# First four jobs of an fp32 transformer-block kernel on un-normalised input, scaled by 1 / rms afterwards

## The reference, cut to what matters

```
def rms_norm(x, g):
    xf = xf * lax.rsqrt(jnp.mean(xf * xf, axis=-1, keepdims=True) + EPS)
    return xf * g

h = rms_norm(x, norm1_g)                      # x: 256 x 1024
z = h @ w_in                                  # 1024 x 7168
a_val, a_gate = split(z[:, :2048])            # 1024 columns each
a = a_val * sigmoid(a_gate)
a = causal_depthwise_conv(a, conv_w, conv_b)  # 31 taps per channel
a = silu(rms_norm(a, conv_norm_g))
```

## Time and profile before

| | us |
|---|---|
| three runs | 917.16, 919.43, 921.28 (median 919.43) |
| the profiled execution | 918.12 |
| its span | 916.3 |
| PE busy | 877.1 (96% of the span) |
| DVE busy | 639.7 (70%) |
| ACT busy | 553.7 (60%) |
| POOL busy | 344.6 (38%) |

### The profile page before, as it was taken

How to read it: one execution, slowest core, us unless ns; L and a number is a source line. 1 busy time by engine, 2 the same in 40 slices (tenths; PEclk the granted TensorE clock), 3 DMA queues, 4 the chain that set the end, 5 groups by cost and what they waited for, 6 DMA issues and landing times.

```text
span 916.3 us, 18118 instructions
## 1 busy us (share of the span) xinstructions
PE 877.1 (96%) x6794; PEld 837.2 (91%) x6794; DVE 639.7 (70%) x1050; ACT 553.7 (60%) x999; POOL 344.6 (38%) x318
## 2 busy tenths in 40 slices
PE   4999999999999999999999998899999999999996
PEld 3998898888899899999999887898899999999996
DVE  5887998975777798777656679945468854444542
ACT  5667778777646576666455674474545755555441
POOL 2699984435432243333111117520013343333111
PEclk9999999999999999999999999999999999999999
DMA  5655554434556366555756352344245476554641
GB/s 200 207 183 184 178 170 126 143 103 136 147 186 190 100 202 201 180 183 166 229 183 176 127 184 79 107 138 132 76 139 176 148 210 186 183 184 160 209 136 46
DMA packets 42310, 146.41 MB, mean 160 GB/s; under 512 B 4704, under 2 KB 7024, under 8 KB 42224
## 3 DMA queue, kind: packets, MB, share of 16 engines
q1 hardware_dynamic: 41472, 143.67, 50.3%
q10 hardware_dynamic: 752, 1.59, 0.5%
HBM read 144.19 MB, written 1.05 MB: 159 GB/s over the span
## 4 chain that ended last, share of the span: by engine, by line
PE 84%; issue 5%; DVE 4%; ACT 3%; POOL 3%; DMA 1%; DVEq 0%; POOLq 0%; ACTq 0%
PE px L502 25%; PE px L503 24%; PE px L504 24%; PE px L544 3%; POOL att L1973 2%; PE px L564 2%; DVE wlo L1307 1%; PE px L573 1%; PE px L508 1%; PE px L509 1%; PE px L510 1%; PE px L552 1%; ACT whi L842 1%; DVE hx L1328 1%; PE px L566 1%
## 5 line engine op out<-in xcount | busy, mean ns | idle before, releaser
L502 PE MATMUL px<-hx,whi 128*128 128x256 f32 x1392 | 404.0, 290 | 8.7 <-DVE hx L1328 6.1
L503 PE MATMUL px<-hx,whi 128*128 128x256 f32 x1392 | 395.4, 284 | 0.0
L504 PE MATMUL px<-hx,wlo 128*128 128x256 f32 x1392 | 395.3, 284 | 0.0
L1307 DVE TENSOR_TENSOR wlo<-raw,whi 128x1024 fp32r<-128x1024 f32 x251 | 329.9, 1322 | 66.3 <-ACT whi L842 65.3
L842 ACT ACTIVATE whi<-raw 128x1024 fp32r<-128x1024 f32 x267 | 279.9, 1051 | 65.6 <-PE px L504 49.9
L502 PEld LDWEIGHTS px<-hx,whi 128*128 128x128 f32 x1392 | 268.3, 193 | 16.7 <-DVE hx L1328 7.4
L503 PEld LDWEIGHTS px<-hx,whi 128*128 128x128 f32 x1392 | 268.8, 193 | 0.4
L504 PEld LDWEIGHTS px<-hx,wlo 128*128 128x128 f32 x1392 | 268.6, 193 | 0.0
L1863 POOL TENSOR_TENSOR CA<-CA,ct 128x256 f32<-128x256 f32 x90 | 86.7, 963 | 54.5 <-ACT ct L909 47.0
L1930 POOL TENSOR_TENSOR fx<-tt,fx 128x256 fp32r<-128x256 f32 x40 | 56.3, 1410 | 129.7 <-ACT fx L1098 124.5
L503 PE MATMUL px<-fx,whi 128*128 128x256 f32 x352 | 99.6, 283 | 0.0
(11 more groups left out here) (281 smaller groups left out, 1303.1 us busy)
## 6 DMA issues: line engine op xcount, KB each, us to landing
raw<-ws SPq DMA_DIRECT2D x267, 512.0 KB, 3.7
tb<-tabs SPq DMA_DIRECT2D x16, 128.0 KB, 2.9
out<-X SPq DMA_DIRECT2D x4, 256.0 KB, 2.4
X<-xs SPq DMA_DIRECT2D x1, 512.0 KB, 4.9
X<-xs ACTq DMA_DIRECT2D x1, 512.0 KB, 5.0
msk<-lmask ACTq DMA_DIRECT2D x1, 448.0 KB, 3.6
vc<-vecs ACTq DMA_DIRECT2D x1, 319.0 KB, 6.8
ug<-pos ACTq DMA_DIRECT2D x1, 128.0 KB, 4.2
```

The source lines that it names most:

```text
L502: e.matmul(b[:, 0:S], H, xh, start=first, stop=False)
L503: e.matmul(b[:, 0:S], H, xl, start=False, stop=False)
L504: m = e.matmul(b[:, 0:S], L, xh, start=False, stop=end)
L1307: e.tensor_tensor(wlo[:, n % NSL, :], raw[:, n % NRAW, :], whi[:, n % NSL, :], ALU.subtract).then_inc(s_lov, 1)
```

## The change

**Jobs on x times the gain.** The first four jobs (ag0, av0, ag1, av1) no longer read the normalised tiles `hx` but `ax`, which holds x times norm1_g split into high (ACT) and low (DVE) parts. `sums("n1")` moves behind ag0 and av0. When 1 / rms is there, DVE multiplies the four PSUM results by it (`early`), ACT takes the tanh of the two gates, and DVE writes CI(0) and CI(1) (`early_gated`). The later twelve jobs read `hx` as before.

**Pieces.** x comes in four DMAs of two tiles. Chunks 0 and 1 come, and are split, in halves of 128 x 512. All of these are on SP's queue in the order of use, and the 9 columns of vectors that the opening needs come in a small DMA of their own. The other 629 columns come behind chunk 2.

**Engines.** POOL instead of DVE adds up the squares, and chunk 3's low part is DVE's instead of POOL's. The normalised tiles and chunks 4 and 5 are woven together in DVE's and ACT's lists.

ACT's list (the early multiplications and gates are called as shown for DVE):

```
-            e.dma_start(X[:, 0:4, :], xv[:, 0:4, :]).then_inc(s_x[0], 16)
-            e.dma_start(vc[:, :], vecs).then_inc(s_vc, 16)
...
+            for i in range(KD):
+                if i % 2 == 0:
+                    e.wait_ge(s_x[i // 2], 16)
+                e.activation(ax[:, i, 0, :], X[:, i, :], ACT.Copy, scale=vec("norm1_g", i)).then_inc(s_xgh, 1)
+                if i in (1, 3):
+                    half_high(0, i // 2)
+            half_high(1, 0)
+            half_high(1, 1)
+            for i in range(KD):
+                square("n1", i, X[:, i, :])
+                if i == 3:
+                    highs(2)
+            highs(3)
+            rms("n1", D)
...
+            early_gate(0)
+            highs(4)
+            early_gate(1)
```

DVE's list:

```
+            for i in range(KD):
+                e.wait_ge(s_xgh, i + 1)
+                e.scalar_tensor_tensor(out=ax[:, i, 1, :], in0=X[:, i, :], scalar=vec("norm1_g", i), in1=ax[:, i, 0, :],
+                                       op0=ALU.mult, op1=ALU.subtract).then_inc(s_xgl, 1)
+                if i in (1, 3):
+                    half_low(0, i // 2)
...
+            def early(key, to):
+
+                e.wait_ge(s_mm, ENDS[key])
+                e.tensor_tensor(to, px_of[key, 0][:, 0:S], rst[:, 0, 0:S], ALU.mult).then_inc(BANK[key, 0][0], 1)
...
+            e.wait_ge(s_rms, 1)
+            early(("ag", 0), sg[:, 0, :])
+            early(("av", 0), CI[:, 0, 30:])
+            scaled("n1", 0, X[:, 0, :], "norm1_g")
+            early(("ag", 1), sg[:, 1, :])
```

The lists of PE, POOL and SP:

```
+            job(("ag", 0), AX, first_gained, rings=(FEW,))
+            job(("av", 0), AX, rings=(FEW,))
             sums("n1")
+            job(("ag", 1), AX, rings=(FEW,))
+            job(("av", 1), AX, rings=(FEW,))
...
+            for i in range(KD):
+                add_square("n1", i)
             low_tiles("n1", hx)
...
+            tiles(0)
+            half_load(0, 0)
+            tiles(1)
+            half_load(0, 1)
+            tiles(2)
+            tiles(3)
+            half_load(1, 0)
+            half_load(1, 1)
+            loads(2)
+            e.dma_start(vc[:, FIRST_VECS:], vecs[:, FIRST_VECS:]).then_inc(s_vc, 16)
```

More of the change, by code:

```diff
@@ L420, in on_gpsimd, with steps, half, gated_half @@
         def on_gpsimd(c):
-            return c < 64 and c % 4 == 3
+            return 4 <= c < 64 and c % 4 == 3
+        def steps(c):
+            return 2 if c < HALVED else 1
         LOW = {}
         for c in range(n_chunks):
-            n = c // 4 if c < 64 else 16
-            LOW[c] = (s_log, c // 4 + 1) if on_gpsimd(c) else (s_lov, c + 1 - n)
+            mine = [d for d in range(c + 1) if on_gpsimd(d) == on_gpsimd(c)]
+            LOW[c] = (s_log if on_gpsimd(c) else s_lov, sum(steps(d) for d in mine))
+        HI = [sum(steps(d) for d in range(c + 1)) for c in range(n_chunks)]
+        def half(h):
+            return slice(h * CW // 2, (h + 1) * CW // 2)
+        def gated_half(i):
+            return (s_ci, i + 1) if i < 2 else BANK[("av", i), 0]
         ACC = {i: px[3][:, S * (n % 2):S * (n % 2) + S] for n, i in enumerate(CONV_V)}
@@ L831, in _, with half_high @@
         def _(e):
-            made = [0]
+            made = [HALVED]
+            def half_high(n, h):
+                e.wait_ge(s_raw[n] if h else s_half[n], 16)
+                e.activation(whi[:, n, half(h)], raw[:, n, half(h)], ACT.Copy).then_inc(s_hi, 1)
             def highs(c):
```

108 lines of the change are left out of this document (71 added, 37 removed).

## The result

| | before | after |
|---|---|---|
| time, us, median (range) | 919.23 (917.16 to 921.28), 4 runs | 929.28 (928.82 to 929.73), 4 runs |
| ratio | | 1.0112, 95% interval 1.0091 to 1.0133 |
| span of the profiled execution | 916.3 | 927.1 |
| granted clock, mean | 0.996 | 0.988 |

The forecast was 917.5, range 914.0 to 920.7. The kernel is slower by 1.1%, and the forecast was wrong in sign and size. PE's work grew by little: 881.0 us against 877.1.

The account below looks back on a forecast made before the run. PE was taken as the bound, with POOL setting the first head sum: PE's gain of 4.4 us was cut to 1.1 (2.0 - 0.9), giving 917.0 or, on the median, 918.3; forecast 917.5, range 914.0 to 920.7.

Parts of the forecast that it names:

- The second wait at the head sums: PE's wait of 0.5 us at 110 us, for the fifth head sum, was to stay as before.
- the view that decides: PE's waits between 20 and 120 us: one row, 1.9 us in front of `head_sums`, where PE waits for POOL.
- The gain of this change is by how much POOL's tap of 35.23 comes forward: POOL's second tap was to come at 33.2, 2.0 us ahead; less 0.9 inside POOL's run, the gain was 1.1.
- The signs that the prediction named: Times to check in the changed profile, including ones-matmuls near 15.5, sixteenth job's end near 60, POOL's first q square near 94.4.
- 1 / rms at 17.7: In the opening: last addition at 15.5, ones-matmuls' end at 16.7, then Ln and Exp; 4.8 us later than before.
- the clock rival: At the first head sum PE's longer wait drops the clock, costing 1.7 to 2.5 us; time 919.1, chance 0.10.
- DVE's list behind 1 / rms: DVE's scalings, tiles and splits after the norm, with waits for ag1 and ACT, were to finish chunk 5's low part at 28.0.
- POOL's tap wait for chunk 9: ACT's copy of chunk 9, landing at 31.7, stood ahead of the product that POOL's second tap needs; tap at 33.2.
- its list between them is fixed: POOL, from its second tap to the first square of q, had fixed work and no row with idle time.
- the norm's lateness, 4.8 us: In the opening 1 / rms came 4.8 us later while PE did ag1; PE was still to gain 4.4 us.
- No advance: In the opening, POOL's additions, the wait for ag1 or chunk 9's slow landing eat the gain; 917.8 to 919.1, chance 0.19.

Follow-up runs that it names:

- e4: The changed kernel with the six additions of squares back on DVE, around the split of chunk 2; 924.95 us, ratio 1.0062.
- e7: The changed kernel with 20 filler matmuls ahead of the norm's ones-matmuls and 16 behind the fourth job; 929.2 us, ratio 1.0112.
- e13: The changed kernel with chunk 6's low part on DVE right behind chunk 5's, ahead of the second gated tile; 928.8 us, ratio 1.0096.
- e12: The kernel before with only the pieces: x in four transfers, chunks 0 and 1 in halves; ratio 1.0001.
- e11: The kernel before with 20 extra DVE additions delaying the first norm, nothing done meanwhile; 928.25 us, ratio 1.0091.
- e9: The changed kernel with x first and whole, additions on DVE, and squares and ones-matmuls ahead of the first jobs; 926.68 us, ratio 1.0075.
- e3: The changed kernel with x in two transfers, the first behind the small vectors on ACT's queue, and chunks 0 and 1 whole; 931.1 us, ratio 1.0127.
- e6: e3 with x's first half asked for ahead of the first vectors on ACT's queue; 930.5 us, ratio 1.0131.
- e2: The kernel before with the low parts of chunks 11 and 15 made by DVE instead of POOL; ratio 0.9993.
- e14: e9 with chunks 11 and 15's low parts on DVE, and chunk 6's low part right behind chunk 5's; 924.7 us, ratio 1.0043.

## Why the prediction was wrong

**Right.** PE's first matmul at 6.76 (about 6). POOL's taps, not PE, set the first head sum, and PE waits longer in front of it (3.29; 3 or more was said). The second wait at the head sums stays (0.49). So the view that decides was found. The sentence "The gain of this change is by how much POOL's tap of 35.23 comes forward" held with the other sign and in part: the second tap went back by 6.4, to 41.66, and the head sum by 8.9. The signs that the prediction named all came out late: ones-matmuls 20.01 (15.5), chunk 5's low part 36.2 (28), sixteenth job 70.03 (60), first square of q 104.36 (94.4).

**Wrong, first: "1 / rms at 17.7".** It was 23.02, and this is 5.3 of the miss. Its parts: the last piece of x landed at 10.4, where 256 KB each 0.65 us gave 7.1 for it, so the first addition began at 13.13 in place of 10.0 (+3.1); six additions took 6.75 in place of 5.5 (+1.25); PE's ones-matmuls and ACT's pair took 3.1 in place of 2.2 (+0.95), because PE had fallen to the slow step in its wait of 4.31. The prediction had no wait at this place and took the fast step; it looked for the clock rival at the first head sum alone. Of the +3.1 about 1 is chance: with the same transfers x was complete at 9.1 to 10.4 in four profiles (after, e4, e7, e13), and POOL's first addition began at 12.23 and 12.71 in e7 and e13. I had weighed the rule of the Trainium skill ("DMA: Bandwidth & Descriptors", "Anatomy of one DMA — SWDGE (gpsimd) path") that a DMA on GpSimd's path has a fixed cost, and had set it aside since large chunks overlap. The pieces' landings, 3.5 us for the first and 7.3 for the last of x, show that the rate of four large chunks isn't that of eight small pieces; whether a cost of each transfer or the shorter rows do it, no run settled. The shorter rows alone don't give the rate of the changed kernel: in e12 the same pieces moved at 367 GB/s between 5.6 and 8.4 us, in the changed kernel at 250.

**Wrong, second: DVE's list behind 1 / rms.** From there to chunk 5's low part I had 10.3, and it took 13.2. The third job ended 3.1 behind 1 / rms (1.8), as PE ran half of it at the slow step; the other 1.5 is spread over the tiles and splits of DVE's list behind it. Then comes a step that the prediction did not have at all. It made POOL's tap wait for chunk 9; the first tap waited for the second gated tile, which stands behind chunk 5's low part and lasted 2.64 beside POOL's split, where I had 0.35 for such a tile, from the kernel before.

**Wrong, third: "its list between them is fixed".** From the first tap to the head sum POOL took 2.55 longer. The fourth tap waited 2.63 for ACT, which waited for chunk 10, and that is 1.9 of it; longer taps are the other 0.64. e13, where that wait is gone, has 1.2 back and loses it ahead of the first tap. It is not the idle time that it has back: POOL's idle time within its run is 6.80 there and 7.08 in after, in smaller waits for ACT's products. What sets ACT's pace there stays open.

**The error behind them.** I put the work for the new jobs where the engines were idle in the trace of before, and took the norm's lateness, 4.8 us, as paid for by the jobs done meanwhile. e11 shows that a late norm costs its full lateness, and that the jobs give back 2.0 of it. e9 shows that the early jobs, with what they bring counted in, cost 4.7 us even with the norm in time. "No advance" (0.19) was the rival that pointed there; it stopped at 919.1, because I let the additions be late by 2.1 at most and had no bound for the sum of all of it. That is why the range failed too.

**The clock rival** came true at its place in most of the kernels of the new order, though not in the profiled execution of the kernel itself. In e9 the wait was 3.30:

```profile
100.89 0.67 PE L594 MATMUL px<-hsq,bd 128*128 128x256 f32 x2 [3.30 <-issue]
...
102.00 0.41 PE L525 MATMUL px<-hx,wlo 128*128 128x256 f32 x1
102.21 0.41 PE L523 MATMUL px<-hx,whi 128*128 128x256 f32 x1
```

The steps are 0.21 from 102.0 to 105.2; in after, behind 3.29, they stay 0.12. The same fall stands there in all of e3 to e9, behind waits of 3.04 to 3.82, and not in e13 (3.00) nor in the seven others (2.59 or less). A fall there costs 15 matmuls 0.09 each: the second head sum follows the first by 4.86 in e9 and by 3.37 in after. At the fifth head sum 1.05 of the 1.5 is left, as the wait of 0.49 there is gone. The prediction had both the place and this deduction right; its 1.7 to 2.5 was too much, because it took the slow stretch to be as long as the opening's, and its chance of 0.10 was too low for the place. Whether the three other executions of the changed kernel fell there no profile shows; their granted clock was 0.982 to 0.984, that of the profiled one 0.988.

The prediction also says that no wait in the trace before is long enough to show such a fall. It had asked only up to 120 us. Timeline of PE in before, later on:

```profile
568.62 1.68 PE L699 MATMUL px<-go 64*128 64x128 f32 x16 [1.37 <-DVE go L1670]
...
571.14 0.41 PE L504 MATMUL px<-hx,wlo 128*128 128x256 f32 x1
571.36 0.41 PE L502 MATMUL px<-hx,whi 128*128 128x256 f32 x1
```

The granted clock was 0.83 between 565 and 575 us, behind waits of 1.26 (at 562.5) and 1.37, the second with sixteen small matmuls behind it. So the row that bore on this rival stood in the trace before, behind a shorter wait than the one forecast.

## What to carry to other kernels

Work put ahead of a norm on every engine's list makes the norm late, and its lateness returned in full here, where the work behind it has no slack. Price the lists of ScalarE, DVE and GpSimd instruction by instruction up to the norm's result before counting what TensorE does meanwhile. Delay that result alone in the old kernel, and the price of lateness is known with one run. When several steps in a row are each taken at their middle, bound their sum too: here every one of them came out late.

## What the runs showed of the hardware

- Between 5.6 and 8.4 us after the start the transfers moved at 250 GB/s in the changed kernel (256 KB each, rows of 2 KB), at 367 in e12 (the same pieces, the vectors in one transfer of 319 KB), and at 418 in the kernel before (512 KB each, rows of 4 KB). From 8.4 to 10.5 it was 387, 408 and 417.
- A transfer of 4.5 KB in rows of 36 bytes takes 3.5 to 4.8 us alone in front. 512 KB behind it on its queue landed at 8.3, where ahead of it they landed at 5.8 (e3, e6; 0.4 of that is the later issue).
- The same start gave the first addition on GpSimd at 13.13, 12.71 and 12.23 in three kernels that differ only behind it (after, e13, e7), so about a microsecond of a start is not to be told from chance.
- The tail behind the first head sum was 820.1 to 825.0 us in 16 kernels that all do the same work there. It goes with the falls of the granted clock in it, most of them worth about 1.5 us of slow steps: 820.1 with one (the execution of before from which I argued), 821.9 to 822.7 with two, 821.4 to 823.9 with three, 823.7 to 825.0 with four. After the same two waits of 0.65 and 0.78 the clock fell in one kernel and not in another. A gain of 2 us at the first head sum is not to be told from this in one execution of the whole (e2, e7).
- A DVE instruction of 0.41 us lasted 2.64 where it started just behind a split of 2.4 us on GpSimd, and one of 1.22 us lasted 3.43 (after, e14). Two of six GpSimd additions of 0.75 us took 1.56 and 1.53 where a DVE split was in hand (after).
